# Output products of the first attention in three rounded products, with the splitting of their weights among the attention's units

## What is computed

```python
mix = concatenate([o_diff, o_mla], axis=-1)       # 256 x 1024: eight heads of 128
# o_diff: rmsnorm over each head's 128 columns, times subln_w * (1 - lam_init)
x = x + ga * (mix @ w_out)                        # w_out: 1024 x 1024
hf = modulate(rmsnorm(x, ffn_norm_w), sf, scf)
x = x + gf * moe(hf, router_w, router_b, w1, b1, w2, b2)   # 32 experts, top 4
```

## Time and profile before

| | us |
|---|---|
| median of 3 runs | 1521.44 |
| the runs | 1519.49 to 1522.17 |
| the profiled execution | 1518.81 |
| its span, first to last instruction | 1517.1 |

### The profile page before, as it was taken

How to read it: one execution, slowest core, us unless ns; L and a number is a source line. 1 busy time by engine, 2 the same in 40 slices (tenths; PEclk the granted TensorE clock), 3 DMA queues, 4 the chain that set the end, 5 groups by cost and what they waited for, 6 DMA issues and landing times.

```text
span 1517.1 us, 17420 instructions
## 1 busy us (share of the span) xinstructions
PE 1394.5 (92%) x6836; PEld 753.3 (50%) x6836; DVE 497.2 (33%) x893; ACT 306.8 (20%) x449; POOL 38.3 (3%) x56
## 2 busy tenths in 40 slices
PE   4998999999899899999898999998999899899998
PEld 2775456434333324334333334343343488698987
DVE  2646434213113112121131131131121534655566
ACT  3405233101101001001011011011010532544451
POOL 1000002100000000000000000000000111000000
PEclk9999999999999999999999999999999998999999
DMA  9309916899999999999999999999999660556540
GB/s 375 125 1 380 386 62 218 359 428 429 429 429 428 429 429 429 429 429 429 429 429 429 429 429 429 429 429 429 429 429 428 253 222 21 196 177 191 191 143 28
DMA packets 62826, 500.01 MB, mean 330 GB/s; under 512 B 6216, under 2 KB 22888, under 8 KB 35072
## 3 DMA queue, kind: packets, MB, share of 16 engines
q1 hardware_dynamic: 59616, 492.85, 78.7%
q0 software_dynamic: 1840, 5.82, 1.2%
q10 hardware_dynamic: 1328, 0.77, 0.2%
HBM read 498.37 MB, written 1.05 MB: 329 GB/s over the span
## 4 chain that ended last, share of the span: by engine, by line
PE 67%; DMA 22%; DVE 6%; issue 3%; ACT 1%; SPq 1%; DVEq 0%; ACTq 0%; PEldq 0%
PE bank L1494 30%; DMA ring<-in_w 20%; PE bank L610 17%; PE bank L648 15%; PE bank L668 2%; DMA ring<-in_w_ada 2%; DVE dk L723 1%; DVE mrows L727 1%; DVE dk L717 1%; PE bank L621 1%; PE bank L656 1%; PE bank L630 1%; PE bank L1676 0%; SPq L567 0%; DVE psum_sum L1219 0%
## 5 line engine op out<-in xcount | busy, mean ns | idle before, releaser
L610 PE MATMUL bank<-ring,xn 128*64 128x512 f32 x2048 | 468.0, 610 | 65.6 <-DMA ring<-in_w 63.9
L610 PEld LDWEIGHTS bank<-ring,xn 128*64 128x64 f32 x2048 | 163.5, 140 | 359.9 <-issue 359.9
L648 PE MATMUL bank<-ring,dq 128*64 128x512 f32 x1024 | 226.8, 595 | 0.0
L712 DVE TENSOR_SCALAR mrows<-bank 128x512 f32<-128x512 f32 x32 | 20.6, 686 | 477.6 <-PE bank L610 477.6
L682 ACT ACTIVATE sq<-mrows 128x512 f32<-128x512 f32 x32 | 19.6, 630 | 774.2 <-DVE mrows L712 774.2
L648 PEld LDWEIGHTS bank<-ring,dq 128*64 128x64 f32 x1024 | 70.6, 137 | 136.5 <-issue 133.8
L736 DVE TENSOR_TENSOR dk<-bank,bc 128x512 f32<-128x512 f32 x32 | 22.1, 692 | 236.2 <-PE bank L648 236.2
L469 DVE TENSOR_TENSOR w_lo<-ring,w_hi 128x2048 fp32r<-128x2048 f32 x34 | 77.7, 2291 | 31.2 <-ACT w_hi L464 31.2
L1494 PE MATMUL bank<-x_hi,w_hi 128*128 128x256 f32 x256 | 73.6, 287 | 1.8 <-DVE h_lo L1376 1.8
L1494 PE MATMUL bank<-h_lo,w_hi 128*128 128x256 f32 x256 | 73.4, 287 | 0.0
L1494 PE MATMUL bank<-x_hi,w_lo 128*128 128x256 f32 x256 | 73.3, 286 | 0.0
(11 more groups left out here) (381 smaller groups left out, 1506.0 us busy)
## 6 DMA issues: line engine op xcount, KB each, us to landing
ring<-in_w SPq DMA_DIRECT2D x192, 2048.0 KB, 17.1
ring<-in_w_ff SPq DMA_DIRECT2D x32, 1024.0 KB, 5.5
ring<-in_w_ada SPq DMA_DIRECT2D x24, 1024.0 KB, 16.4
ring<-in_w_out SPq DMA_DIRECT2D x8, 1024.0 KB, 10.2
ring<-in_w_in SPq DMA_DIRECT2D x8, 992.0 KB, 27.0
ring<-in_w_in SPq DMA_DIRECT2D x8, 640.0 KB, 11.3
ring<-in_w_ple_gate SPq DMA_DIRECT2D x4, 1024.0 KB, 4.8
xc<-in_ctx SPq DMA_DIRECT2D x1, 1024.0 KB, 5.0
```

Source lines behind the costliest of these rows:

```text
L610: m = pe.matmul(banks[bank_no][mine(i), :], gathered[:, k, mine(i)], rows_of(at + i, 2)[:, k % 2, q * 512:(q + 1) * 512], start=k == 0, st ...
L648: m = pe.matmul(banks[OUT_BANKS[c]][mine(i), :], actT[:, k, mine(i)], rows_of(8 + 2 * j + i, 4)[:, r, c * 512:(c + 1) * 512], start=k == 0 ...
L712: dve.tensor_scalar(gs[:, half * 512:half * 512 + 512], banks[GATE_BANKS[half]][:], LIMIT, None, ALU.min)\
```

## The change

The output products are computed with `mm3`. The turned operand is written as `mix_hi` (rounded; in place of `mixT`) and `mix_lo` (the rest; over the values `dv`). For pairs 0 and 1 VectorE does both, for 2 and 3 ScalarE rounds and VectorE takes the rest. Each weight chunk of `w_out` gets a ring number of its own behind it, `w_out_hi`, which isn't loaded: ScalarE rounds the chunk into it in two halves of 128x1024, one behind each of the value steps 5 to 12, and GpSimd writes the rest over the loaded chunk, in halves too, ahead of its router load. TensorE waits for both halves of a pair. `FRONT` has 42 numbers, `ring_freed` rises by 2 per weight pair, and all expert and `BACK` chunks move by four slots. ScalarE's roots go from value step 9 to 13, VectorE's scalings from 12 to 14; the sums of squares stay at 9.

```diff
-W_OUT = [("w_out", j) for j in range(4)]
+W_OUT = [(kind, j) for j in range(4) for kind in ("w_out", "w_out_hi")]
@@
+def landings(slot, before):
+
+    return sum(1 for n in range(slot, min(before, N_FRONT), SLOTS) if FRONT[n][0] != "w_out_hi")
@@
+OUT_ROUNDED_FROM = 5
@@
+        mix_hi = over("mix_hi", [P, KD, T], "hT")
+        mix_lo = over("mix_lo", [P, KD, T], "dv")
+        out_hi = {j: over(f"out_hi{j}", [P, SLOT], "ring", SLOT_OF["w_out_hi", j] * SLOT) for j in range(4)}
+        out_lo = {j: over(f"out_lo{j}", [P, SLOT], "ring", SLOT_OF["w_out", j] * SLOT) for j in range(4)}
@@
             for chunk in FRONT:
-                load_chunk(sp, chunk)
+                if chunk[0] != "w_out_hi":
+                    load_chunk(sp, chunk)
@@
+            for j in range(4):
+                for half in range(2):
+                    cols = slice(half * 1024, half * 1024 + 1024)
+                    pool.wait_ge(sem("out_rounded"), 2 * j + half + 1)
+                    step(pool.tensor_tensor(out_lo[j][:, cols].bitcast(F32R), slot(("w_out", j))[:, cols], out_hi[j][:, cols],
+                                            ALU.subtract), "out_split", wait=False)
             wait_read(pool, "mixT0")
@@
-                elif what == "value" and u == 9:
+                elif what == "value" and 0 <= u - OUT_ROUNDED_FROM < 8:
+                    j, half = divmod(u - OUT_ROUNDED_FROM, 2)
+                    cols = slice(half * 1024, half * 1024 + 1024)
+                    if half == 0:
+                        ring_wait(act, ("w_out", j))
+                        act.wait_ge(sem("ring_freed"), AFTER["w_out_hi", j])
+                    step(act.activation(out_hi[j][:, cols].bitcast(F32R), slot(("w_out", j))[:, cols], ACT.Copy), "out_rounded",
+                         wait=False)
+                if what == "value" and u == 13:
 
                     act.wait_ge(sem("ms_done"), 3)
                     step(act.activation(stat[:, 48:56], stat[:, 40:48], ACT.Sqrt), "root_done")
             for j in (2, 3):
                 b = take(act, f"mixT{j}")
-                step(act.activation(mixT[:, 2 * j:2 * j + 2, :], b[:].rearrange("p (k t) -> p k t", k=2), ACT.Copy),
-                     tile=f"mixT{j}")
+                step(act.activation(mix_hi[:, 2 * j:2 * j + 2, :].bitcast(F32R), b[:].rearrange("p (k t) -> p k t", k=2),
+                                    ACT.Copy), "mix_rounded", wait=False)
@@
-                act.wait_ge(moe("ring_freed", MAIN), freed_by(PAIRS - 1, 18 + n, MAIN))
+                act.wait_ge(moe("ring_freed", MAIN), freed_by(PAIRS - 1, 14 + n, MAIN))
@@
-                if what == "value" and u == 12:
+                if what == "value" and u == 14:
                     dve.wait_ge(sem("root_done"), 3)
@@
             for j in range(2):
-                b = take(dve, f"mixT{j}")
-                step(V.tensor_scalar(mixT[:, 2 * j:2 * j + 2, :], b[:].rearrange("p (k t) -> p k t", k=2),
-                                     vecT[:, 11:12], None, ALU.mult), tile=f"mixT{j}")
+                src = take(dve, f"mixT{j}")[:].rearrange("p (k t) -> p k t", k=2)
+                of = (slice(None), slice(2 * j, 2 * j + 2))
+                step(V.tensor_scalar(mix_hi[of].bitcast(F32R), src, vecT[:, 11:12], None, ALU.mult))
+                step(V.scalar_tensor_tensor(out=mix_lo[of].bitcast(F32R), in0=src, scalar=vecT[:, 11:12], in1=mix_hi[of],
+                                            op0=ALU.mult, op1=ALU.subtract), tile=f"mixT{j}")
+            for j in (2, 3):
+                src = take(dve, f"mixT{j}")[:].rearrange("p (k t) -> p k t", k=2)
+                dve.wait_ge(sem("mix_rounded"), j - 1)
+                of = (slice(None), slice(2 * j, 2 * j + 2))
+                step(V.tensor_tensor(mix_lo[of].bitcast(F32R), src, mix_hi[of], ALU.subtract), tile=f"mixT{j}")
@@
-                    n_ = ("w_out", j)
                     if t == 0:
-                        ring_wait(pe, n_)
+                        pe.wait_ge(sem("out_split"), 2 * j + 2)
                         wait_read(pe, f"mixT{j}")
-                    w = slot(n_).rearrange("p (k n) -> p k n", k=2)
+                    w = [v[:].bitcast(F32R).rearrange("p (k n) -> p k n", k=2) for v in (out_hi[j], out_lo[j])]
                     for n in range(2):
                         for kk in range(2):
                             k = 2 * j + kk
-                            m = mm(bw[t, n][:], mixT[:, k, t * P:(t + 1) * P], w[:, kk, n * 512:(n + 1) * 512],
-                                   k == 0, k == KD - 1)
+                            m = mm3(bw[t, n][:], [v[:, k, t * P:(t + 1) * P].bitcast(F32R) for v in (mix_hi, mix_lo)],
+                                    [v[:, kk, n * 512:(n + 1) * 512] for v in w], k == 0, k == KD - 1)
                         if j == 3:
                             m.then_inc(full(f"wo{t}_{n}"), 1)
                         elif t == 1 and n == 1:
-                            m.then_inc(freed, 1)
+                            m.then_inc(freed, 2)
@@
-                    pe.sem_inc(freed, 1)
+                    pe.sem_inc(freed, 2)
```

More of the change, by code:

```diff
@@ L95 @@
     if _n < N_BEFORE:
-        SLOT_OF[_c], USE_OF[_c], AFTER[_c] = _n % SLOTS, _n // SLOTS + 1, _n - SLOTS + 1
+        SLOT_OF[_c], USE_OF[_c], AFTER[_c] = _n % SLOTS, landings(_n % SLOTS, _n + 1), _n - SLOTS + 1
     else:
@@ L99 @@
         _s, _last = FREED_BY_PAIR[_m % BACK_SLOTS]
-        SLOT_OF[_c], USE_OF[_c] = _s, len(range(_s, N_FRONT, SLOTS)) + _m // BACK_SLOTS + 1
+        SLOT_OF[_c], USE_OF[_c] = _s, landings(_s, N_FRONT) + _m // BACK_SLOTS + 1
         AFTER[_c] = _last + 1
@@ L1002, in _ @@
                 if t == 0:
-                    act.wait_ge(moe("ring_freed", MAIN), freed_by(PAIRS - 1, 18 + AHEAD, MAIN))
+                    act.wait_ge(moe("ring_freed", MAIN), freed_by(PAIRS - 1, 14 + AHEAD, MAIN))
             for n in range(AHEAD, FIRST_OUT2):
```

## The result

The changed kernel takes 1521.44 us (median of 12 runs, 1518.77 to 1524.31), the kernel before 1518.39 (12 runs beside them, 1516.72 to 1522.17): ratio 1.0018, interval 1.0010 to 1.0026. That is 2.7 us slower by the ratio and 3.0 between the medians, about the 0.2% that the chances were counted by. The forecast was 1515.3 us, a gain of 5 to 7.2, in a range from 1512.6 to 1518.8. The three runs from which it started are three of the twelve, and their median (1521.44) lies 3.0 us above that of all; set against 1518.39 the forecast would have been 1512.3. The profiled executions are 1524.31 (span 1522.6) after and 1518.81 (span 1517.1) before.

The account below looks back on a forecast made before the run. The expert loop was taken to run at its transfers' pace, so time saved in the chain ahead comes off the end. 5.3 + 1.8 - 1.1 = 6.0 (6.1 by timeline) gave 1515.3 us, range 1512.6 to 1518.8.

Parts of the forecast that it names:

- The products: Output products ahead of the loop: 96 at 232.5 ns, 22.3 us in place of 27.6, a gain of 5.3.
- The roots: Attention's end: roots at step 13 save a table load on the path, so TensorE goes on 1.8 us earlier.
- The rounding on ScalarE: Eight weight copies of 1.05 us behind steps 5 to 12: the first seven cost nothing in ScalarE's idle time.
- the tail's 1.1: Before the output products: late root, eighth rounding and second VectorE operation per pair take back 1.1 of 1.8 us.
- GpSimd: Eight weight subtractions of 2.36 us during the attention: they keep pace, and contention with VectorE was taken as nothing.
- rival A: Contention: VectorE's two-SBUF-input operations wait for GpSimd's subtractions, costing 2.3 us, so 1517.6 us; 15 in 100.
- D: Clock: stays up in the router stage, 1513.5 us, 8 in 100; or falls near 209 us, 1517, 5 in 100.
- E: Output products' operands come so late, through the tail's chain of steps, that the gain is eaten: 1520 to 1521; 5 in 100.
- Behind the loop: Four second-block chunks are issued later, behind the last pair, but land by 1200 us: cost nothing, cover 3.6 us.
- The ring ahead of the loop: Two more expert blocks load after the attention, done by 261.2 us, before the loop's first slots: cost nothing, cover 2.6.
- B: Ring ahead of the loop fills a little late, 1 to 3 us of overrun: about 1517.3 us; 13 in 100.
- C: Prefetch ahead of the loop decides: the two blocks' 9.8 us are not hidden at all, 1525.1 us; 4 in 100.

Follow-up runs that it names:

- e6_late_roots: Kernel before with only the roots moved to value step 13 and the scalings to 14: ratio 0.9997 to the kernel before.
- e8_rearranged: Changed kernel with GpSimd's subtractions kept away from VectorE's instructions with two SBUF operands, and loads behind the loop held back: 1511.49 us, 0.9954 of the kernel before.
- e2_split: Changed kernel with each GpSimd subtraction split into four of 256 columns: one run, 1519.81 us.
- e4: Changed kernel with the load queue held before w_in2 chunk 4 until TensorE passes the loop's end: ratio 0.9992 to the kernel before.
- e11: Changed kernel with the load queue held at w_in2 chunk 6, so two chunks still load behind the loop: one run, 1516.63 us.
- e12: Changed kernel with the load queue held at w_in2 chunk 7, so three chunks still load behind the loop: one run, 1515.30 us.
- e3: Kernel before with only the changed kernel's ring numbering, so four chunks load behind the loop: 1522.61 us, 1.0028 of the kernel before.
- e5: Kernel before with the changed kernel's ring numbering and the load queue held until TensorE passes the loop's end: ratio 1.0006 to the kernel before.
- e1_gap: Changed kernel with roundings at value steps 4 to 8 and 10 to 12, none at 9: ratio 1.0008 to the kernel before.
- e7_gap_late_loads: Changed kernel with no rounding at step 9 (one at 4 instead) and loads held until TensorE passes the loop's end: 1514.36 us, 0.9980 of the kernel before.

## Why the prediction was wrong, point by point

- **The products, right.** 22.3 us forecast, 22.6 measured, 27.6 before.
- **The roots, right but mis-sized.** 1.8 forecast, 1.28 measured (e6_late_roots). The exponential came when I said, but TensorE then waited elsewhere in the tail, for copies and for the scalings.
- **The rounding on ScalarE and the tail's 1.1, right.** With GpSimd out of the sums' way the tail is 18.30, against 17.19 with late roots alone: 1.11. In e8_rearranged, with the eighth rounding out of the tail, 0.66 are left.
- **GpSimd, the step that failed first.** I took nothing for the contention and gave rival A 15 in 100. The price of A came out right, 2.3 us, but not its parts: I had 1.8 at the sums and 0.5 at the scalings; the sums lost 2.1 and 0.3, and the scalings, at 1.42 us as before, nothing. In e2_split it was 2.0. The chance was wrong, because the row nearest to it has a PSUM operand on VectorE's side, and so no bearing: such instructions go on undisturbed also beside 11.6 us of GpSimd. "No row shows it" should have made A the likeliest case, with the rule that the forecast named from the Trainium skill beside it: the traces agree with that rule. The Trainium skill, "SBUF — State Buffer", section SBUF: two separate sides, says more: the ports that VectorE and GpSimd share are an exclusive lock for the whole instruction, and a VectorE instruction with two SBUF inputs needs it against any GpSimd instruction that reads SBUF. 2.35 beside 2.35, 0.69 beside a quarter and 1.00 beside a copy of 1.06 bear it out.
- **The clock, mis-placed.** D had a fall in the tail at 5 in 100 and for gaps near 209. It fell at 202, behind the gap that the contention made, and cost up to some 3.1 us (23.8 us of tail twice, 21.7 twice, with none of it 20.3 in e2_split). A and D were treated as separate. The clock fell in all four executions with undivided subtractions beside the sums (changed, e4, e11, e12), in one of three that have the old roots and no subtraction (e3, not before and e5), and in none of the other six. So they go together; that the gap itself is the cause is argued and not shown. The outcome is that of E, products started too late for a gain, but by A and D and not by the chain of steps that E named.
- **Behind the loop, the step that failed second.** "Cost nothing, cover 3.6 us" asked only when the chunks were wanted, and they were in time: the last landed at 1203.4, and ScalarE rounds from 1207.42. What I did not ask is what else must pass the DMA engines at 1194 to 1202: the code of TensorE behind the loop. That the loads cost the time is shown both ways, by adding them (e3_turn) and by holding them back (e4, e5); that it is TensorE's code they hold up is inferred from the packets. They cost 1.6 to 2.6 us in the stretch behind the loop, and in four of the five kernels with all four loads there some 1.8 more in the second block (316.0 to 316.3 in place of 314.3), whose clock stays lower. In medians: 4.1 (e3_turn against before), 3.6 and 4.0 (the changed kernel and e1_gap against their pairs with late loads).
- **The ring ahead of the loop, right.** B and C did not come about.

The sum of what was shown: -5.0 - 1.3 + 1.1 for what was forecast, + 2.3 and 1 to 3 for the contention and its clock, + 4 behind the loop: 2 to 4 us slower, measured 2.7. What stays open is why the second block's clock stays low after late starts in four kernels and not in the fifth (e1_gap); it was not tried. The profiled execution of e1_gap (1513.94 us) is the fastest of its twelve, 4.5 below their median, so this may be the execution and not the kernel.

## What to carry to other kernels

Work given to GpSimd is free only beside VectorE instructions that don't read two SBUF operands: list those in its shadow, however small, and put GpSimd's instructions between them. Splitting them in four left VectorE's wait at 2.0 us of 2.3 in the one run that tried it. Where a loop or a branch ends, ask not only when a load is wanted but what it stands before: bulk loads issued just ahead of it delayed the code of the engine that went on. And a wait of one or two microseconds on TensorE is to be priced together with the clock that it may cost.

## What the hardware did that I had not expected

- A VectorE instruction on a single column (128x1, 0.22 us) waited 2.1 us for GpSimd's subtraction (e7_gap_late_loads), and GpSimd is held up too: two subtractions took 5.11 us in place of 4.72 when VectorE's stood between them (e1_gap).
- TensorE's next instructions behind the loop came 2.5 to 3.1 us after an instruction packet of 0.02 MB, which bulk loads push back: with 4 loads of 0.66 MB it came amid the last of them, some 2.8 us later against the mixing than with none (7.0 us behind its start in place of 4.2).
